# One more block of seven products in each sweep of the down projection, and their order changed

## The reference, cut to what matters

```python
def conv_ffn(h, w_up, conv_w, w_down):
    up = h @ w_up
    upp = jnp.pad(up, ((0, 0), (CONV_WIDTH - 1, 0), (0, 0)))
    conv = sum(upp[:, i:i + s] * conv_w[i] for i in range(CONV_WIDTH))
    gate, val = conv[..., :D_FF], conv[..., D_FF:]
    return (jax.nn.gelu(gate, approximate=True) * val) @ w_down
...
        x = x + rms_norm(conv_ffn(h2, w_up, conv_w, w_down), ln_post_ffn)
```

## Time and profile before

| | |
|---|---|
| median of 3 runs | 1574.82 us |
| profiled execution | 1575.19 us |
| span of its trace | 1573.4 us |
| TensorE / VectorE / ScalarE busy, share of the span | 99% / 83% / 55% |
| DMA, mean over the span | 233 GB/s |
| mean granted TensorE clock | 0.998 of full speed |

### The profile page before, as it was taken

The page is one execution under the profiler, slowest core; times in us unless marked ns, Lnnn a source line. Parts: engine busy times, 40 slices in busy tenths (PEclk is TensorE's granted clock), DMA queues, the critical chain, the costliest instruction groups (busy, mean ns, idle before and its releaser), DMA issues.

```text
span 1573.4 us, 24737 instructions
## 1 busy us (share of the span) xinstructions
PE 1563.7 (99%) x8622; PEld 1355.0 (86%) x8622; DVE 1306.9 (83%) x1842; ACT 860.5 (55%) x1150; POOL 2.0 (0%) x12
## 2 busy tenths in 40 slices
PE   9999999999999999999999999999999999999998
PEld 7888888888888888888888888888888888888886
DVE  6566677678797798888888888888888999989997
ACT  6544554446565654444444444444544567666764
POOL 0000000000000000000000000000000000000000
PEclk9999999999999999999999999999999999999999
DMA  9886455556666467776777767777677688868984
GB/s 371 267 232 198 162 181 167 187 161 191 193 257 215 147 202 237 227 232 212 230 232 226 233 212 236 228 227 231 212 241 227 239 312 320 308 257 321 315 312 156
DMA packets 247474, 366.37 MB, mean 233 GB/s; under 512 B 6752, under 2 KB 211200, under 8 KB 246528
## 3 DMA queue, kind: packets, MB, share of 16 engines
q1 hardware_dynamic: 243728, 360.70, 69.0%
q10 hardware_dynamic: 3696, 5.00, 1.3%
HBM read 339.20 MB, written 26.48 MB: 232 GB/s over the span
## 4 chain that ended last, share of the span: by engine, by line
PE 99%; DMA 0%; DVE 0%; ACT 0%; SPq 0%; issue 0%; DVEq 0%
PE ps L1692 44%; PE ps L1696 23%; PE ps L1785 15%; PE ps L1985 10%; PE ps L1835 3%; PE ps L1798 1%; PE ps L1707 1%; PE ps L1712 0%; DMA raw<-in_w_in_dram 0%; PE ps L1924 0%; PE ps L1905 0%; PE ps L1917 0%; PE ps L1934 0%; PE ps L2048 0%; DVE arena L1668 0%; PE ps L2081 0%
## 5 line engine op out<-in xcount | busy, mean ns | idle before, releaser
L1692 PE MATMUL ps<-actT,w_hi 128*128 128x512 f32 x3072 | 715.0, 390 | 0.0
L533 ACT ACTIVATE w_hi<-raw 128x1024 fp32r<-128x1024 f32 x420 | 432.7, 1054 | 474.2 <-PE ps L1696 234.2
L1692 PEld LDWEIGHTS ps<-actT,w_hi 128*128 128x128 f32 x3072 | 569.5, 188 | 112.0 <-issue 0.2
L983 DVE TENSOR_TENSOR w_lo<-raw,w_hi 128x1024 fp32r<-128x1024 f32 x422 | 506.4, 1224 | 163.2 <-ACT w_hi L533 160.0
L1696 PEld LDWEIGHTS ps<-actT,w_lo 128*128 128x128 f32 x3072 | 372.4, 188 | 10.2 <-issue 1.7
L1696 PE MATMUL ps<-actT,w_lo 128*128 128x256 f32 x3072 | 378.4, 279 | 0.0
L1785 PE MATMUL ps<-w_hi,xs 128*128 128x512 f32 x672 | 183.9, 389 | 0.0
L1785 PEld LDWEIGHTS ps<-w_hi,xs 128*128 128x128 f32 x672 | 126.1, 188 | 26.1
L1985 PE MATMUL ps<-actT,s_parts 128*128 128x512 f32 x480 | 124.9, 390 | 0.0
L1546 DVE SCALAR_TENSOR_TENSOR arena<-arena,convw 128x256 f32<-128x256 f32 x256 | 106.7, 480 | 0.0
L1985 PEld LDWEIGHTS ps<-actT,s_parts 128*128 128x128 f32 x480 | 89.4, 188 | 19.9 <-DVE actT L1321 1.8
(11 more groups left out here) (189 smaller groups left out, 1013.7 us busy)
## 6 DMA issues: line engine op xcount, KB each, us to landing
raw<-in_w_up_dram SPq DMA_DIRECT2D x128, 1024.0 KB, 6.0
raw<-in_w_down_dram SPq DMA_DIRECT2D x64, 1024.0 KB, 6.6
raw<-in_w_in_dram SPq DMA_DIRECT2D x58, 1024.0 KB, 5.3
token_forms<-xs SPq DMA_DIRECT2D x30, 768.0 KB, 7.8
s_parts<-token_forms SPq DMA_DIRECT2D x32, 704.0 KB, 4.9
raw<-in_w_o_dram SPq DMA_DIRECT2D x16, 1024.0 KB, 5.2
raw<-in_w_a_out_dram SPq DMA_DIRECT2D x8, 1024.0 KB, 5.3
raw<-in_w_b_out_dram SPq DMA_DIRECT2D x8, 1024.0 KB, 5.4
```

Source lines behind the costliest of these rows:

```text
L533: act.activation(w_hi[:, h % RING, :], raw[:, h // 2, h % 2 * HALF:(h % 2 + 1) * HALF], ACT.Copy)\
L983: dve.tensor_tensor(lo, raw[:, h // 2, h % 2 * HALF:(h % 2 + 1) * HALF], w_hi[:, h % RING, :].bitcast(F32), ALU.subtract).then_inc(lo_read ...
L1692: return pe.matmul(ps[:, bank + c, :], w_hi[:, h % RING, at:at + P], actT[:, k, :, :].rearrange("p a s -> p (a s)"), start=start, stop=stop)
```

## The change

It gives each sweep a seventeenth seven and puts them in another order. Written with S for a seven and O for an ordinary unit, the middle of `down0` was S O SS O S O SS O S O SS O S O SS O S O SS O S (units 3 to 28), and becomes S O SS O SS O S O SS O SS O S O SS O SS O S O S (units 3 to 29). In `down1` the same pattern stands one unit earlier. The last seven moves from unit 28 to 29 and from 27 to 28.

```diff
 FIRST = (3, 2)
-DOWN_SEVENS = ((3, 5, 6, 8, 10, 11, 13, 15, 16, 18, 20, 21, 23, 25, 26, 28),
-               (2, 4, 5, 7, 9, 10, 12, 14, 15, 17, 19, 20, 22, 24, 25, 27))
+DOWN_SEVENS = ((3, 5, 6, 8, 9, 11, 13, 14, 16, 17, 19, 21, 22, 24, 25, 27, 29),
+               (2, 4, 5, 7, 8, 10, 12, 13, 15, 16, 18, 20, 21, 23, 24, 26, 28))
+
```

## The result

The changed kernel takes 1581.06 us, the median of 6 runs (1580.63 to 1581.31), against 1574.91 for the kernel before (6 runs, 1574.67 to 1575.16). The ratio is 1.0039, with a 95% interval from 1.0029 to 1.0048: slower by 6.15 us. Forecast were 1580.6 us and +5.8. The profiled execution took 1581.22 us and its span 1579.4, 6.0 longer than the span before. The lines are numbered one higher from here on, as the changed list is one line longer: L1321 of before is L1322, L811 is L812.

The account below looks back on a forecast made before the run. TensorE was taken to set the end, with VectorE nearly full at 98%. Terms -1.36 + 7.44 - 0.20 - 0.1 = +5.8 us gave 1580.6 us, range 1577.4 to 1583.4, chance 0.74.

Parts of the forecast that it names:

- The saving of a seven: On TensorE, a seven in an ordinary unit's place saves 0.68 us; two added give -1.36 us.
- The two rates: Down projection, VectorE against TensorE: falls back 1.96 us in a seven, gains 3.17 in an ordinary unit.
- the ceiling of 0.57: Behind a pair's second seven VectorE is always 0.57 us ahead, since ScalarE rounds only as TensorE frees buffers.
- lead: Time from VectorE finishing BT2 of a seven to TensorE's first load of the last products that need it.
- The stop: At the second seven of a pair one ordinary unit behind another pair, TensorE is held up 1.24 us.
- two needs: To avoid stopping in a seven, the pair needs 0.53 us of lead and BT needs 0.9.
- Six places: Three places "SS O SS" in each sweep, each stopping TensorE for 1.24 us: +7.44 us.
- small stops: Stops of 0.05 us in the other pairs, falling from 10 to 6: -0.20 us.
- The edits costed at nothing: Loads and start of down1 stay covered, at no cost; end of down1 has 0.4 us cover, taken as -0.1.
- A: VectorE's lead carries over pairs, leaving it short only 0.3 us per cycle: +0.4 us, 1575.2; chance 0.12.
- B: TensorE's path alone counts at each second seven behind O SS: -1.7 us, 1573.1; chance 0.06.
- C: A later seven or a load behind a stop, or the end, is late too: about +9, 1584; chance 0.08.

Follow-up runs that it names:

- the split: Changed kernel with the middle products split, so the wait for VectorE's rest of BT stands three matmuls later: 1579.03 us.
- the narrow sum: Changed kernel with one VectorE weight-block sum made 64 instead of 512 columns wide in the six stopping units, result not the reference's: 1578.26 us.
- the alternating order: Against the kernel before, 17 sevens per sweep with pairs and lone sevens in turn, one ordinary unit between: 1574.98 us.
- the kernel with the order of before: Kernel before with split middle products, early s_parts load, and the rest of b22 made by GpSimd instead of VectorE: 1584.62 us.

## Why the prediction was right

**The saving of a seven** on TensorE, 0.68 us, was not measured alone. The changed order with 17 and with 16 per sweep differ by 1582.22 - 1581.06 = 1.16 us. By the traces that is two savings, 1.36, and 0.12 at the end of down1, less the 0.37 of the load at its start: 1.11. So fewer matmuls do give time back here, although weight loads are busy for only 82% of a cycle.

**The two rates** (VectorE falls back 1.96 us in a seven, gains 3.17 in an ordinary unit) and the ceiling of 0.57 behind a pair held in the place that matters: unit 8 has a lead of 1.59 in the changed kernel too (BT2 ends at 1280.55, load at 1282.14). The stop is 1.24 as forecast, and the traces with the split and with the narrow sum show that its two parts are two needs. Their sizes were off by 0.07 in opposite directions (1.02 and 0.31 for 0.95 and 0.38), because the signal from VectorE to TensorE took 0.11 at the pair and not the 0.05 seen at BT. In the sum this cancels by the mechanism; in the split kernel, where only the pair's part is left, it shows.

**Six places.** One place cost 1.2 and six cost 7.2, with four small stops fewer, so the count of places explains both.

**The edits costed at nothing.** The end of down1 gave back 0.12, as taken, and had more cover than the 0.4 forecast: VectorE is done at 1562.38 and TensorE's load comes at 1563.53. At the start of down1 the forecast named the wrong load: it looked at raw, and gave the s_parts load 5.9 us of cover from its cadence in mid-sweep and its median landing of 4.3 us. There it is issued right behind two others and takes 7.3 to 9.6 us to land, about twice the median that the forecast went by. In the kernel before 2.1 us of cover are left of that, in the change none. Its 0.37 us are as much as lies between forecast (+5.8) and result (+6.15); two other differences of 0.3 us at units 20, 21 and 24 of down1 cancel.

**Rivals.** A (the deficit is spread) would give +1.8 us for the changed order with 16 sevens, 0.3 in each of its six cycles, and B (TensorE's path alone) nothing or less. That kernel took +7.2, so both fall. A matters for one more reason. The two orders with 17 sevens are equal in count but not in density: the change packs five sevens into eight units, the alternating order three into five, as before. By the forecast's numbers VectorE is then short by 0.3 us in a cycle of the one and has 0.5 to spare in a cycle of the other. Density thus explains 1.8 us at most, and the stops the rest; the kernel with one moved seven shows a stop without any added density over the sweep. C (more stops) is not seen at the six places or at the end. The one wait for a load, at the start of down1, stands behind no stop.

The prediction prices the case without stops once at -1.4 and once, under B, at -1.7. The second also counts the small stops and the end of down1.

**What is open:** why the pair 20 and 21 of down1 waits 0.45 instead of 0.17 in the four traces with the changed order, 17 sevens and unsplit products. ScalarE's rounding of BT starts there 0.27 us later behind its releaser than elsewhere; the next stop is shorter by about as much (0.32 against 0.28), so that it costs nothing in the sum. It is open too why the load at the start of down1 takes longer in some traces.

## What to carry to other kernels

Where two engines are both nearly full in a stage (here 98% and 100%), it pays to judge a list of units of two kinds by a ledger, unit by unit: what the second engine gains and loses against the first, the ceiling that shared buffers set on its lead, and the lead that each wait needs. Totals say how many expensive units fit; the ledger says where, and here the order was worth 6 us at equal count. Where one engine must wait for the other to hand a buffer back, as ScalarE does in the second seven of each pair, the lead falls to a fixed value (0.57 here), and slack from before that place does not help behind it.

## What the runs showed of the hardware

GpSimd was no free helper for VectorE on this float32 data: a 128 x 512 subtraction took it 1.4 to 2.0 us beside VectorE (32 times in the kernel with the order of before), and the VectorE operation at the same time grew by 1.0 to 1.1 us, where a 128 x 512 subtraction takes VectorE 0.69. In the profile the releaser named beside a wait for several semaphores was another engine than the one that was late, in all six long waits; making the named instruction shorter by 0.75 us changed nothing but the label. A 704 KB load that landed in 4.3 us in mid-sweep (median) took 7.3 to 9.6 us where it was issued right behind two others.
